# Filling work moved between the stages of a decoder step: its first weights split one stage earlier, its casts on ScalarE, matmuls kept for the stage ends, the output matrix on GpSimd

## What is computed

```python
xn   = rms_norm(x) * g                     # [T, 1024]
q, k, v, z, f, gates... = xn @ w_in        # 512-column groups of w_in; the three gate branches take 6
# fox branch: 8 heads of 64, softmax attention with a forget bias from cumulated log gates
# hgrn2 branch: 4 heads of 128, a gated linear recurrence in 64 chunks (4 heads x 16 tiles of 128 tokens)
# memory branch: 4 heads of 128, attention over memory keys/values mem @ w_mk, mem @ w_mv
y = rms_norm(x + (sum_b sigmoid(gate_b) * (branch_b @ w_b)) @ w_o)
# sample rows: the same with attention over paged caches and a carried recurrent state
```

## Time and profile before

| | before |
|---|---|
| median of 3 runs | 3064.44 us (3054.81 to 3074.55) |
| the profiled execution | 3058.63 us, span 3056.9 us |
| granted TensorE clock, mean | 0.961 of full |
| PE busy | 2802.7 us, 92% of the span, 13880 matmuls |
| DVE / ACT / POOL busy | 1583.8 / 1036.8 / 811.6 us |
| DMA | 528.44 MB, 173 GB/s |

### The profile page before, as it was taken

One profiled execution on the slowest core, in us unless ns is written; L12 is line 12 of the kernel. 1 busy time (PEld: TensorE's weight loads), 2 busy tenths in 40 slices (PEclk: granted clock), 3 DMA queues, 4 the chain that ended last, 5 costly groups with the idle time before them and its releaser, 6 DMA issues. The chain is left out here.

```text
span 3056.9 us, 38630 instructions
## 1 busy us (share of the span) xinstructions
PE 2802.7 (92%) x13880; PEld 2295.1 (75%) x13880; DVE 1583.8 (52%) x3023; ACT 1036.8 (34%) x1972; POOL 811.6 (27%) x846
## 2 busy tenths in 40 slices
PE   7899998999995989999779999999999977999998
PEld 5678776667774878787658888888887865888887
DVE  5415676343443446556426665666664545444544
ACT  2211111332321334344225555555554234232322
POOL 6058885344244252533350020020020000000000
PEclk9999998999997999999889999999999998999999
DMA  5587778566544657666575455554443545433331
GB/s 168 222 257 230 233 249 277 186 176 185 174 136 143 200 194 244 205 219 200 176 223 155 138 147 160 156 160 142 139 139 114 198 170 173 131 107 117 116 109 49
DMA packets 292430, 528.44 MB, mean 173 GB/s; under 512 B 110398, under 2 KB 135551, under 8 KB 270991
## 3 DMA queue, kind: packets, MB, share of 16 engines
q1 hardware_dynamic: 239967, 408.13, 42.5%
q0 software_dynamic: 16656, 53.36, 6.0%
q10 hardware_dynamic: 35616, 64.47, 5.5%
HBM read 413.19 MB, written 112.68 MB: 172 GB/s over the span
## 5 line engine op out<-in xcount | busy, mean ns | idle before, releaser
L2452 PE MATMUL fill_out<-fill_w_hi,fill_x 128*128 128x512 f32 x2112 | 739.1, 414 | 94.3 <-POOL fill_w_lo L2545 45.0
L2452 PEld LDWEIGHTS fill_out<-fill_w_hi,fill_x 128*128 128x128 f32 x2112 | 393.7, 193 | 174.4 <-POOL fill_w_lo L2545 58.9
L2452 PE MATMUL fill_out<-fill_w_lo,fill_x 128*128 128x512 f32 x1056 | 438.1, 415 | 0.0
L461 DVE TENSOR_TENSOR fox_pt_lo<-fox_turned,fox_pt_hi 128x512 fp32r<-128x512 f32 (+1 forms) x320 | 194.8, 609 | 157.1 <-ACT fox_pt_hi L408 155.3
L2086 ACT ACTIVATE in_stage<-in_out 128x512 f32<-128x512 f32 (+1 forms) x119 | 70.9, 597 | 593.7 <-PE in_out L99 546.3
L408 ACT ACTIVATE fox_pt_hi<-fox_turned 128x512 fp32r<-128x512 f32 (+1 forms) x320 | 170.1, 531 | 300.8 <-PE fox_turned L358 299.1
L447 DVE CUSTOM_DVE_ANT_0 fox_probs<-fox_scores,fox_bias 128x512 f32<-128x512 f32 (+2 forms) x320 | 187.5, 608 | 93.1 <-PE fox_scores L347 50.6
L2543 POOL CAST fill_w_hi<-fill_raw 128x512 fp32r<-128x512 f32 x80 | 51.5, 644 | 678.5 <-PE fill_out L2463 643.5
L2452 PEld LDWEIGHTS fill_out<-fill_w_lo,fill_x 128*128 128x128 f32 x1056 | 204.6, 194 | 30.5
L97 PE MATMUL in_out<-x_first,ring_hi 128*128 128x512 f32 x512 | 201.0, 393 | 7.4 <-POOL ring_lo L2007 7.4
L99 PE MATMUL in_out<-x_first,ring_hi 128*128 128x512 f32 x512 | 200.5, 392 | 0.0
(11 more groups left out here) (356 smaller groups left out, 5932.8 us busy)
## 6 DMA issues: line engine op xcount, KB each, us to landing
fill_x<-x_tiles SPq DMA_DIRECT2D x132, 1024.0 KB, 5.4
dc_slot<-in_cache_fox_k_dram SPq DMA_DIRECT2D x128, 256.0 KB, 3.9
dc_slot<-in_cache_fox_v_dram SPq DMA_DIRECT2D x128, 256.0 KB, 3.1
in_raw<-in_w_in_dram POOLq DMA_DIRECT2D x104, 256.0 KB, 4.0
plain<-fill_stage ACTq DMA_DIRECT2D x96, 256.0 KB, 5.4
mf_gate<-plain SPq DMA_DIRECT2D x96, 256.0 KB
turned<-in_stage ACTq DMA_DIRECT2D x64, 256.0 KB, 3.9
fill_raw<-in_w_in_dram POOLq DMA_DIRECT2D x64, 256.0 KB, 3.0
```

The costliest lines, as they stand in the source:

```text
L461: dve.tensor_tensor(pt_lo[:, b, skip:BANK], bank_of(st)[:, skip:BANK], pt_hi[:, b, skip:BANK].bitcast(F32), ALU.subtract).then_inc(turned_ ...
L2452: ins = pe.matmul(self.out[n % self.OUTS][:], x, w, start=(k == 0 and term == 0), stop=(ends and term == 2))
```

## The change

- **Ring.** The ring of 16 is held in two arrays: `keep` (places 4 to 7 and 12 to 15) and `rest`. `keep` lives on after the projection stage as the filling's weights. In ticks 104 to 111 the projection stage also loads and splits the 8 slices of the filling's first group into `keep`. The recurrence starts with them split.
- **Projection.** The cast is ScalarE's (`high`, L2158), before the evictions of the tick for slices that must wait for the last unit of a group, after them for the others. GpSimd has the loads and the subtract (`low`). Three raw buffers for two. In the first pass two slices a tick. The decode's `middle` steps m = 2, 3, 4, 5 come one or two ticks later.
- **Recurrence.** Masks are built behind unit 0's preparation, with a semaphore of their own that DVE waits for at the first product with them; SyncE loads x tile 0, unit 0, x tile 1, unit 1, v. The filling's casts are ScalarE's here. 1340 matmuls over all 138 slots for 1600 over 134, and 96 in four slots behind the last chunk.
- **Fox.** 144 matmuls in the first slots for 100, 1472 for 1396, 22 at the end around the last `out` and `back`. TensorE waits for the constants at the first score. The second head's queries and values are loaded at the first score, not before.
- **Memory.** 16 matmuls before its first wait; one more gate group stands before the memory groups.
- **Merge.** w_o's slices are loaded, cast and subtracted by GpSimd alone, two raw buffers in the space of `gains`, which is loaded after them.

```diff
-MATMULS = {"recur": 1600, "first": 100, "fox": 1396}
+MATMULS = {"recur": 1340, "recur_last": 96, "fox_first": 144, "fox": 1472, "fox_last": [10, 12], "memory_first": 16}
...
-    PASSES, STAGES, OUTS, RAWS = 2, 4, 4, 2
+    PASSES, STAGES, OUTS, RAWS = 2, 4, 4, 3
...
+        def split_at(m):
+            n, k = divmod(m, KT)
+            if ring_before[m] is not None and ring_before[m] // KT == n - 1:
+                return n * U - 1
+            return (n - 1) * U + (k // 2 if n < G else k)
...
+                def low(m):
+                    hi, lo = w_ring.at(ring_at[m])
+                    pool.wait_ge(cast, m - KT + 1)
                     pool.tensor_tensor(lo, raw[m % RAWS][:], hi.bitcast(F32), ALU.subtract).then_inc(split, 1)
+                    if m + RAWS < SLICES:
+                        pool.wait_ge(split, m - KT + 1)
                         load_raw(m + RAWS)
...
+                def high(m):
+                    act.wait_ge(raw_loaded[m % RAWS], 16 * ((m - KT) // RAWS + 1))
+                    ring_free(act, m)
+                    act.activation(w_ring.at(ring_at[m])[0], raw[m % RAWS][:], ACT.Copy).then_inc(cast, 1)
+
                 for t in range(TICKS):
+                    for m in range(KT, SLICES):
+                        if split_at(m) == t and t % U == U - 1:
+                            high(m)
                     for e in events_at(t):
                         evict(e)
...
-        if m == 3:
+        if m == 4:
             dve.wait_ge(self.spread_done, a + 1)
...
+                fill.sync_start(sp)
                 load_unit(0)
+                fill.sync_next(sp)
+                load_unit(1)
                 load_v(0)
-                fill.sync_start(sp)
-                for u in range(1, HH):
+                for u in range(2, HH):
                     load_unit(u)
...
-                    if n + AHEAD < SPLITS:
-                        fill.gpsimd_first(pool, n + AHEAD, SPLITS)
+                    if n == 2 - AHEAD:
+                        build_masks()
...
-    steps += [("out", *quads[-1]), ("back", *quads[-1])]
+    TAIL = FILLS + 2 * FH * J_HEAD
+    steps += [("out", *quads[-1]), ("fill", TAIL), ("back", *quads[-1]), ("fill", TAIL + 1)]
...
+    def high_by_scalar(self, act, n):
+        self.wait_slice(act, n)
+        act.activation(self.w_hi[:, n % KT, :], self.raw[n % self.RAWS][:], ACT.Copy).then_inc(self.cast, 1)
...
+            @block.gpsimd
+            def _(pool):
...
+                for i in range(2):
+                    load(i)
+                for i, (kk, n) in enumerate(last_slices):
+                    at = slice(n * BANK, (n + 1) * BANK)
+                    pool.wait_ge(late_loaded[i % 2], 16 * (i // 2 + 1))
+                    pool.tensor_copy(w_hi[:, kk, at], late_raw[i % 2]).then_inc(late_split, 1)
+                    pool.wait_ge(late_split, 2 * i + 1)
+                    pool.tensor_tensor(w_lo[:, kk, at], late_raw[i % 2], w_hi[:, kk, at].bitcast(F32), ALU.subtract
+                                       ).then_inc(late_split, 1)
+                    if i + 2 < len(last_slices):
+                        pool.wait_ge(late_split, 2 * i + 2)
+                        load(i + 2)
...
-                            pe.wait_ge(w_split, MERGE_W + (n + 1) * KT)
+                            pe.wait_ge(late_split, 2 * (n + 1) * KT)
```

More of the change, by code:

```diff
@@ L516, in walk, with tail_slots @@
             post(BLOCKS - 1, piece)
+            tail(piece)
     def slots_of(n):
         return 2 * (n + AHEAD), 2 * (n + AHEAD) + 1
+    def tail_slots(piece):
+        first = 2 * (len(chunks) + AHEAD) + piece * TAIL // PIECES
+        return range(first, first + TAIL // PIECES)
     with ExitStack() as ctx:
@@ L620, in _, with tail @@
                     load_z(n)
[L621 to L622 removed]
+                def tail(piece):
+                    for slot in tail_slots(piece):
+                        fill.sync(sp, slot)
                     store(BLOCKS - 1, piece)
+                walk(nothing, nothing, nothing, nothing, extra, tail)
                 sp.wait_ge(state_ready, len(chunks))
@@ L745, in extra, with tail @@
                     fill.scalar(act, slots_of(n)[1])
-                walk(prepare, early, take, post, extra)
+                def tail(piece):
+                    for slot in tail_slots(piece):
+                        fill.scalar(act, slot)
+                walk(prepare, early, take, post, extra, tail)
             @block.vector
@@ L857, in extra, with tail, attend_memory @@
                     fill.tensor(pe, slots_of(n)[1])
-                walk(nothing, pairs, sums, nothing, extra)
-def attend_memory(nc, core, queries, mem_k, mem_v, z_mem, gated, last, fill, matmuls, needed):
+                def tail(piece):
+                    for slot in tail_slots(piece):
+                        fill.tensor(pe, slot)
+                walk(nothing, pairs, sums, nothing, extra, tail)
+def attend_memory(nc, core, queries, mem_k, mem_v, z_mem, gated, last, fill, matmuls, first_matmuls, needed):
     ST = NM // P
@@ L1069, in extra, with __init__, at, kept @@
                 def extra(u):
-                    fill.scalar(act, u)
+                    fill.scalar(act, u + 1)
                     paged.scalar(act, u)
+                fill.scalar(act, 0)
                 walk(score, nothing, nothing, extra)
+class Ring:
+    def __init__(self, keep, rest):
+        self.keep, self.rest = keep, rest
+    def at(self, place):
+        half = KT // 2
+        pair, n = (self.keep, place - half) if place // half % 2 else (self.rest, place)
+        return [t[:, n // KT * half + n % KT, :] for t in pair]
+    @staticmethod
+    def kept():
+        half = KT // 2
+        return [*range(half, KT), *range(KT + half, 2 * KT)]
 class SampleRows:
@@ L2098, in _ @@
                             store(e - 1)
+                    for m in range(KT, SLICES):
+                        if split_at(m) == t and t % U < U - 1:
+                            high(m)
                     sums.scalar(act, t)
@@ L2560, in gpsimd @@
                 if self.until(slot) <= last_use < self.until(slot + 1):
-                    self.split_slice(pool, g * KT + k)
+                    yield g * KT + k
+    def gpsimd(self, pool, slot):
+        for n in self.slices_at(slot):
+            if not self.cast_by_scalar:
+                self.high(pool, n)
+            self.low(pool, n)
 class PagedEnd:
@@ L2778, in _ @@
                     if t == 0:
-                        for i in range(MERGE_W, len(slices)):
-                            load_w(i)
                         load_x(0)
```

286 lines of the change are left out of this document (155 added, 131 removed).

## The result

The changed kernel takes 3051.85 us (median of 14 runs, 3041.76 to 3055.55), the kernel before beside it 3073.57 (14 runs, 3054.81 to 3085.77): ratio 0.9932, 95% interval 0.992 to 0.9945. It is 0.7% faster; 3.4% were forecast. The profile before, from which the forecast was made, is of a run of 3058.63 us, 15 under the median that 14 runs give.

The account below looks back on a forecast made before the run. TensorE is busy 92% of the span, with the loss at stage borders; -20 - 25 - 9 - 28 - 6.5 - 14 = -102.5 us from 3058.6 gives 2956, about 2961 in the median's measure, stated as 2960, range 2912 to 3012.

Parts of the forecast that it names:

- "same": Whole kernel: the outcome of a time not told from the kernel before, within some 1% (31 us); chance 0.04.
- Projection, -20: Projection stage: casts on ScalarE, two slices a tick and a third raw buffer end low-part waits; -20 us (-3 to -30).
- Start of the recurrence, -25: Projection-recurrence border: x tile 0 first, weights already split, masks later; -25 us (-18 to -33).
- Group changes, -9: Filling's weight-group changes in the recurrence: casts on ScalarE gain 3 us a change; -9 us (-3 to -28).
- End of the recurrence and fox start, -28: Recurrence-fox border: 96 matmuls fill the idle stretch, constants' wait and loads move; -28 us (-15 to -40).
- Fox to memory, -6.5: Fox-memory border: 22 matmuls at the end and 16 ahead of the `mem_v` wait cover waiting; -6.5 us (-3 to -11).
- Merge, -14: Merge: w_o's loads, casts and subtracts on GpSimd end the 15.5 us wait for `mf_m_lo`; -14 us (-19 to +4).
- The recurrence's own chain: Rival, recurrence: its chain becomes the bound at 6.7 us a chunk, 32 us come back, 2992 us; chance 0.17.
- DVE held by GpSimd: Rival, merge: DVE's branch splits wait for the shared port, turning -14 into +9, 2983 us; chance 0.08.
- ScalarE held by loads: Rival, projection and recurrence: casts waiting for raw slices hold evictions and decays, 208 us, 3164 us; chance 0.03.
- Its signs: Profile after: filling, low-part and `mf_m_lo` waits gone, constants about 5; wrong if cast or x-tile waits exceed 30 us.

Follow-up runs that it names:

- f1: The kernel before with one edit, two slices a tick split by GpSimd in the projection's first pass: ratio 1.0085 to the kernel before.
- e1: The changed kernel with one slice a tick in the projection's first pass again: 3045.75 us, ratio 0.9906 to the kernel before.
- e5: The changed kernel with the projection's casts on GpSimd again, two slices a tick kept: ratio 0.9918 to the kernel before.
- e6: The changed kernel with the projection's casts on GpSimd and one slice a tick in the first pass: 3034.7 us, ratio 0.9881 to the kernel before.
- e2: The changed kernel with the decode's softmax steps back at their earlier ticks: 3047.43 us, ratio 0.9915 to the kernel before.
- f2: The kernel of e9 with the decode's softmax steps at their earlier ticks again: 3007.83 us, ratio 0.9798 to the kernel before.
- e9: The changed kernel with the projection's casts on GpSimd, one slice a tick in the first pass and three raw buffers for the filling: 3010.03 us, ratio 0.9821.
- e8: The changed kernel with three raw buffers for the filling instead of two: 3033.56 us, ratio 0.9881 to the kernel before.
- e12: The changed kernel without the 96 filling matmuls behind the recurrence's last chunk, done in fox instead: 3051.89 us, ratio 0.9953 to the kernel before.
- e10: The changed kernel with GpSimd starting w_o's splits only after DVE's 24 branch-weight subtracts: 3060.24 us, ratio 0.9971 to the kernel before.

## Why the prediction was wrong

The sign was right, the size was not: 22 us for 104 forecast, and 3051.85 lies outside 2912 to 3012. By the prediction's own measure, that some 1% can't be told from nothing, 22 us is its "same", which had 0.04. Point by point:

- **Projection, -20, measured +11 to +21: the step that failed, by its sign.** The waits of L2037, it says, "are slices late for a first pass with one slice a tick; two a tick and a third raw buffer end them", and so 20 us were to go. The waits for low parts ended (1.6 for 20.0). What wasn't asked is what else stands in GpSimd's queue: the decode's products, with DVE and then TensorE behind them. f1 prices this one edit at 21 to 26 us, e1 at some 8 us in the changed kernel, e5 and e6 together at 11. The cast on ScalarE costs 4 us beside it (e5 against the changed kernel) and some 7 without it (e6 against e1), and nearly all of that is the border. The softmax steps are not the cause (e2, f2). With both edits taken back the projection is as long as before, so its 20 us were not there to win this way.
- **Start of the recurrence, -25, measured -14.** x tile 0 did land 5.1 us after its issue, for 5.4 forecast, and no split was waited for. 4.7 us went into GpSimd's later DRAIN ahead of it, 9.97 for 4 into tile 2, which is issued at 992.77 behind the loads of the preparation and lands 15.2 us later. In e9, with the short barrier, the stretch takes 27.6, so -19.
- **Group changes, -9, measured +3.** "There are still two raw buffers [...] the load bounds": right, and undersized. Undersized was the loss before, too: the chunk behind the one of 15.17 us took 12.26, so a group change cost 13 us and not 7.9. The wait for the load is ScalarE's now, with evictions and `hg_k_rows` behind it. e8's third buffer shows it: -11 here and -8 in the fox stage, where the forecast had no term at all and the changed kernel lost 11 (waits for `keep_lo` of 11.4 us).
- **End of the recurrence and fox start, -28, measured -18 to -21.** The constants' move and the loads' order gave 13 to 16 (e12 against before), the 96 matmuls not 21.7 but 6. SyncE's part of a filling slot wasn't counted: its wait in a tile's issue ahead of the last store. x tiles are waited for 17.9 us here, where 4 were given back for them.
- **Fox to memory, -6.5, measured -6.5.** The memory stage then lost 5, which stays unexplained.
- **Merge, -14, measured -9 in the changed kernel, -7.5 alone.** The 15.5 us went as forecast; DVE's slower subtracts took about 8 back (60.8 in e10 for 68.8). "By the row, only GpSimd got slower" was an inference from one row of GpSimd's; DVE's instructions in the same stretch weren't read. The Trainium skill, "SBUF — State Buffer", section "Who interferes with whom", has the rule of a shared, exclusive port pair, and e10 agrees with it: 1179 ns beside GpSimd, 691 without.
- **The rivals.** The recurrence's own chain isn't the bound: a chunk takes 6.02 to 6.25 us where no group changes, as forecast (6.2). DVE held by GpSimd (0.08) came true in part, without turning the term's sign. ScalarE held by loads (0.03, priced at 208 us) came true at two group changes for 19 us in all. The range was too narrow because each rival was weighed as if alone, and the terms' low ends as if they could not come together. Together they are -3 - 18 - 3 - 15 - 3 + 4 = -38, and the measured -22 lies short even of that, since the projection's sign was wrong.
- **Its signs.** Waits for ScalarE or x tiles of over 30 us were to show the forecast wrong, and they appeared: x tiles alone 46.5, of which 24.9 ahead of the first sum, and 20.4 for `fill_stage`. The wait for constants (5.4) and `mf_m_lo` came out as it says. The list of largest waits left out two that the page before has, 25.7 us for `np_normed` in the first stage and 21.8 for `mf_g_in` in the merge; the change aims at neither, and both are still there after (25.8 and 19.1).

What stays open: why GpSimd's DRAIN behind the projection takes 10 us, why the projection of e6 and e9, the same code, ended at 963.5 and 944.4, and why two slices a tick cost 21 to 26 us in the kernel before (f1) and give back only 8 to 11 in the changed one (e1, e6).

## What to carry to other kernels

Before work is moved earlier in a queue, list what stands behind it in that queue and who waits for that: the wait that one sees (low parts, 8.6 us) was cheaper than the one that it made (26 us). An engine with a second duty must not stand in a wait for a load; give the load another buffer first, then move the work (in the recurrence the third buffer and ScalarE's casts give 20 us together, the casts alone, with two buffers, 6). Ahead of a stage's end, let each engine's last work end early: GpSimd's end of the block came 10 us behind its last instruction. Where every low end of a sum has the same cause, queues shared by stages, the range must let them come together.

## What the runs showed of the hardware

GpSimd's and DVE's subtracts of two SBUF operands at the same time: in the merge DVE's goes from 691 ns (e10, and before) to 1179 (after), while GpSimd's 16 go from 1274 ns (e10, begun behind DVE's weight subtracts) to 1364. At the end of the recurrence before it was GpSimd's that went from 1.26 to 2.11 us, beside DVE instructions of 1024 elements (those at the same time start at 1513.83 and 1515.50). So either of the two can pay most of it; what decides which isn't shown.

GpSimd's DRAIN at the end of the projection's block ends 10.0 to 10.1 us after its last instruction, in all 20 profiles.
